# The MLP of a hybrid decoder layer: Strassen's scheme for its up-projection, and a reordered norm phase

## What is computed

```python
def rmsnorm(x, w):
    y = x * lax.rsqrt(jnp.mean(jnp.square(x), axis=-1, keepdims=True) + EPS)
    return y * w

h = concatenate([meta_tokens, x])
mix = hybrid_mixer(rmsnorm(h, norm_mix_pre), w_in, ...)       # starts with rmsnorm(...) @ w_in
h = h + rmsnorm(mix, norm_mix_post)
f = jnp.square(jax.nn.relu(rmsnorm(h, norm_mlp_pre) @ w_mlp_up)) @ w_mlp_down   # 1024 -> 4096 -> 1024
h = h + rmsnorm(f, norm_mlp_post)
return h[:, 16:]
```

## Time and profile before

| | before |
|---|---|
| median of 3 runs | 1740.33 us (1739.41 to 1749.16) |
| the profiled execution's own time | 1749.06 us |
| its span, first to last instruction | 1746.8 us |
| PE busy | 1638.4 us (94%) |
| DVE busy | 821.7 us (47%) |
| POOL busy | 802.8 us (46%) |
| ACT busy | 491.3 us (28%) |
| mean granted TensorE clock | 0.977 of full |

### The profile page before, as it was taken

How to read it: one execution, slowest core, us unless ns; L and a number is a source line. 1 busy time by engine, 2 the same in 40 slices (tenths; PEclk the granted TensorE clock), 3 DMA queues, 4 the chain that set the end, 5 groups by cost and what they waited for, 6 DMA issues and landing times.

```text
span 1746.8 us, 23031 instructions
## 1 busy us (share of the span) xinstructions
PE 1638.4 (94%) x8311; PEld 1402.6 (80%) x8311; DVE 821.7 (47%) x1404; ACT 491.3 (28%) x1002; POOL 802.8 (46%) x775
## 2 busy tenths in 40 slices
PE   2999999987999999789999999999999999999998
PEld 2999998866887878568887778888888888888886
DVE  5465515155666666647778774222222222222226
ACT  4222312233444444345554443020202020101022
POOL 4452544144565643734321315646464646464623
PEclk8999999998999999889999999999999999999999
DMA  5343622226355433578878642111111111111113
GB/s 175 87 123 91 190 72 61 66 74 170 117 152 152 142 116 103 153 248 296 293 277 284 247 145 90 50 49 49 47 51 46 53 43 54 42 54 42 54 67 150
DMA packets 165542, 208.43 MB, mean 119 GB/s; under 512 B 18912, under 2 KB 117056, under 8 KB 165472
## 3 DMA queue, kind: packets, MB, share of 16 engines
q1 hardware_dynamic: 165472, 207.52, 37.2%
HBM read 138.16 MB, written 69.30 MB: 119 GB/s over the span
## 4 chain that ended last, share of the span: by engine, by line
PE 64%; DVE 7%; ACT 2%; DMA 1%; issue 1%; POOL 1%; SPq 0%; DVEq 0%; ACTq 0%
PE ps L2303 20%; PE ps L2289 20%; PE ps L2187 5%; PE ps L1454 4%; PE ps L1380 2%; PE ps L1429 2%; PE ps L1400 1%; DVE pTlo L1625 1%; PE ps L2143 1%; PE ps L1440 1%; PE ps L1426 1%; PE ps L2167 1%; DVE stat L1610 1%; PE ps L1386 1%; PE ps L1427 1%
## 5 line engine op out<-in xcount | busy, mean ns | idle before, releaser
L164 POOL TENSOR_TENSOR ring<-stage,zero 128x512 fp32r<-128x512 f32 (+2 forms) x191 | 207.0, 1084 | 324.2 <-PE ps L2303 108.8
L2303 PE MATMUL ps<-ring,f1hi 128*128 128x512 f32 x1024 | 315.2, 389 | 0.0
L2289 PE MATMUL ps<-hmThi,ring 128*128 128x512 f32 x960 | 299.2, 390 | 3.5 <-DVE ring L2651 3.5
L166 POOL TENSOR_TENSOR ring<-stage,ring 128x512 fp32r<-128x512 f32 (+2 forms) x191 | 250.4, 1311 | 14.9
L2303 PEld LDWEIGHTS ps<-ring,f1hi 128*128 128x128 f32 x1024 | 192.2, 188 | 39.9
L2289 PEld LDWEIGHTS ps<-hmThi,ring 128*128 128x128 f32 x960 | 180.7, 188 | 41.5 <-DVE ring L2651 4.0
L2303 PE MATMUL ps<-ring,f1lo 128*128 128x512 f32 x512 | 199.2, 389 | 0.0
L2668 DVE TENSOR_TENSOR acc<-ps,acc 128x512 f32<-128x512 f32 x128 | 88.0, 691 | 212.1 <-PE ps L2303 210.2
L2289 PE MATMUL ps<-hmTlo,ring 128*128 128x512 f32 x480 | 187.2, 390 | 0.0
L2461 ACT ACTIVATE relu<-ps 128x512 f32<-128x512 f32 x64 | 38.2, 597 | 518.0 <-PE ps L2289 518.0
L2659 DVE TENSOR_TENSOR ps<-ps,relu 128x512 f32<-128x512 f32 x64 | 44.8, 700 | 218.4 <-ACT relu L2461 218.4
(11 more groups left out here) (376 smaller groups left out, 3399.8 us busy)
## 6 DMA issues: line engine op xcount, KB each, us to landing
stage<-w_mlp_up SPq DMA_DIRECT2D x64, 256.0 KB, 2.6
stage<-w_mlp_down SPq DMA_DIRECT2D x64, 256.0 KB, 2.6
stage<-w_in SPq DMA_DIRECT2D x40, 256.0 KB, 2.7
stage<-w_out SPq DMA_DIRECT2D x32, 256.0 KB, 4.5
xt<-x SPq DMA_DIRECT2D x8, 512.0 KB, 7.0
d_xT<-xdT SPq DMA_DIRECT2D x8, 512.0 KB, 3.3
d_x<-x_tok SPq DMA_DIRECT2D x8, 512.0 KB, 4.6
d_zT<-zs SPq DMA_DIRECT2D x16, 256.0 KB, 2.3
```

Of the source, the lines that this page charges most:

```text
L164: pool.tensor_tensor(hi, src, k.zero[:, 0:1].broadcast_to([P, width]), ALU.add).then_inc(k.sem(fam + "_hi"), 1)
L166: pool.tensor_tensor(lo, src, hi.bitcast(F32), ALU.subtract).then_inc(k.sem(fam + "_cut"), 1)
L2289: mm = pe.matmul(ps[:, bank_of(n, first), :], block_w[:, P * j:P * j + P], HM[b][:, kk, at], start=(kk == 0 and a == 0 and b == 0), stop=( ...
L2303: mm = pe.matmul(ps[:, 2 + n % 4, :], f1[a][:, j, P * t:P * t + P], W[b][:, HALF + 2 * j + c, :], start=(j == 0 and a == 0 and b == 0), st ...
```

## The change

**Up-projection.** The first group of 512 features stays as it was. The other 3584 are taken in 14 groups of 256 (`SUB`), a loop of PE in which the up-projection of a group is seven products of quarters (the Winograd form of Strassen's scheme). The weight's quarters are A11, A12, A21, A22 (512 of the width by 128 features), the quarters of the normed input B11 and so on (512 of the width by 512 positions). Each product is 4 slices x 3 passes = 12 matmuls of 512 columns, where eight such products did it before. The sums of weight quarters S1 to S4 are made by POOL for each group, the sums of input quarters T1 to T4 once, by DVE, during the first group (`t2_first` ... `t4_parts`). Banks X, Y, Z, V collect the products; three intermediate results are copied out by ACT (`kept`) and added by DVE (`total`). The down-projection of a group has 16 banks of 2 slices x 3 passes = 6 matmuls. The tiles go in the order 4 to 7, 0 to 3. In the first group the down banks are copied instead of added and their order is changed. The weights of a group are loaded as quarters (256 KB each, in runs of 512 bytes) after the products that use the same place.

**Norm phase.** x tiles are loaded first, five of them ahead of the first weights; the tables that are used later come last. The square's table is loaded with the root's by an early root. ACT scales four of the eight tiles, DVE the other four. The learned positions are turned early. PE works on the projection of f = 0 and of a third of f = 1 between the transposes (`part`) and does the rest of f = 0 before the block ends. POOL cuts 16 blocks there, not 8 (`AHEAD`).

Some semaphores are merged or renamed elsewhere; that moves nothing. The core of the diff:

```diff
-AHEAD = KD
+AHEAD = 2 * KD
@@ phase_norm, scalar
+            for t in ORDER[:FIRST]:
+                square(t)
+            root(0, slice(0, FIRST))
+            square(4)
+            scaled(1)
+            scaled(3)
+            square(5)
+            square(6)
+            high(0)
+            square(7)
+            high(1)
+            root(1, slice(FIRST, NT + 1))
+            high(2)
+            scaled(5)
+            scaled(7)
@@ phase_norm, tensor
+            for n in range(6, 2 * KD):
+                turn(n)
+                if n < 6 + KD:
+                    part(0, 0, n - 6, 0)
+                    part(1, 0, n - 6, 3)
...
+            for q in (1, 2):
+                for kk in range(KD):
+                    mm = part(0, q, kk, q)
@@ phase_rest
+    PRODUCTS = ("A11", "S1", "S2", "S4", "S3", "A12", "A22")
+    BANK_OF = {"A11": X, "S1": Y, "S2": X, "S4": Y, "S3": X, "A12": Z, "A22": X}
+    RESULTS = ((0, 1, Y, "S2"), (1, 1, V, "S1"), (0, 0, Z, "A11"), (1, 0, X, None))
@@ gpsimd
+            def up_quarters(G):
+                scaled(G, "S3", 1)
+                scaled(G, "A22", 2)
...
+                combined(G, "S1", "S3", "A22", ALU.add, 2)
+                scaled(G, "A11", 4)
+                combined(G, "S2", "S1", "A11", ALU.subtract, 4)
+                combined(G, "S3", "A11", "S3", ALU.subtract, 5)
+                scaled(G, "A12", 7)
+                combined(G, "S4", "A12", "S2", ALU.subtract, 7)
+                for n, q in enumerate(PRODUCTS):
+                    pool.wait_ge(sem("x_hi"), of_sub(G, 9, n + 1))
+                    pool.tensor_tensor(mats[q][1][:, :, :], raw(q), mats[q][0][:, :, :].bitcast(F32), ALU.subtract).then_inc(sem("x_lo"), 1)
@@ tensor
+            def product(G, n):
+                q = PRODUCTS[n]
+                pe.wait_ge(sem("x_lo"), of_sub(G, 11, n + 1))
+                if q == "A11":
+                    pe.wait_ge(sem("v_sq_out"), 2 + UP + of_sub(G, 4))
+                if q in ("S1", "S2", "S3", "A22"):
+                    pe.wait_ge(sem("x_tlo"), table(MOVING[q], 1) + 1)
+                if q in ("S2", "S4", "S3"):
+                    pe.wait_ge(sem("x_kept"), of_sub(G, 3, n - 1))
+                if q == "A22":
+                    pe.wait_ge(sem("x_sum"), of_sub(G, 3, 2))
...
+                for kk in range(4):
+                    for a, b in PASSES:
+                        mm = pe.matmul(bank, mats[q][a][:, kk, :], MOVING[q][b][:, kk, :], ...)
-            with pe.Fori(1, GRPS) as g:
-                for n in range(UP):
-                    up_bank(g, n, False)
-                down_group(g)
+            with pe.Fori(FIRST_SUB, SUBS) as G:
+                for n in range(7):
+                    product(G, n)
+                down_sub(G)
@@ scalar
+            def sub(G):
+                weights_high(G)
+                if isinstance(G, int):
+                    for c in range(2):
+                        table_high(T4, c)
+                kept(G)
+                down_high(G)
+                result_high(G)
@@ vector
+            for n in range(11, DN):
+                down_first(n)
+            dve.wait_ge(sem("x_tlo"), table(T2, 1) + 1)
+            for c in range(2):
+                t4_parts(c)
+            for c in range(2):
+                table_low(T4, c)
+            up_sub(FIRST_SUB)
```

More of the change, by code:

```diff
@@ L281, in root, with high @@
                 act.activation(s_[:, part], v[:, part], ACT.Sqrt).then_inc(sem("sqrt"), 1)
-            for t in range(NT // 2):
-                square(t)
-            root(0, slice(0, NT // 2))
-            act.wait_ge(sem("c_in"), 80)
-            after = {1: 4, 3: 5, 4: 6, 5: 7, 7: 8}
-            for n in range(2 * KD):
+            def high(n):
                 half, kk = n // KD, n % KD
@@ new lines, in down_sub @@
+            def down_sub(G):
+                pe.wait_ge(sem("x_lo"), of_sub(G, 11, 11))
+                for n in range(DN):
+                    t, c = TILES[n // 2], n % 2
+                    if n in (0, DN // 2):
+                        pe.wait_ge(sem("v_sq_out"), 2 + UP + of_sub(G, 4, 2 if n == 0 else 4))
+                    pe.wait_ge(sem("v_added"), ADDED + of_sub(G, DN, max(n - 3, 0)))
+                    for j in range(2):
+                        for a, b in PASSES:
+                            mm = pe.matmul(ps[:, 2 + n % 4, :], fs[a][:, j, P * t:P * t + P], half(wd[b][:, j, :], c),
+                                           start=(j == 0 and a == 0 and b == 0), stop=(j == 1 and a == 1))
@@ new lines, in kept, with down_high @@
+            def kept(G):
+                for n, q in enumerate(("A11", "S1", "S2")):
+                    act.wait_ge(sem("v_up"), UP + of_sub(G, 7, n + 1))
+                    act.activation(result_room(1, *KEPT[q]), ps[:, BANK_OF[q], :], ACT.Copy).then_inc(sem("x_kept"), 1)
+            def down_high(G):
+                for j in range(2):
+                    act.wait_ge(sem("x_wd"), of_sub(G, 32, 32))
+                    act.activation(wd[0][:, j, :], wd_plain[:, j, :], ACT.Copy).then_inc(sem("x_hi"), 1)
@@ L2731, in _, with t2_first @@
                 dve.wait_ge(sem(f"m_sent{u}"), 16 * NT // 2)
-            for n in range(FT, UP):
-                square(0, n)
-                for t in {FT: (0, 1), FT + 1: (2, 3), UP - 1: (4, 5, 6, 7)}.get(n, ()):
-                    dve.memset(acc[:, t, :], 0.0).then_inc(sem("acc_set"), 1)
-            dve.wait_ge(sem("acc_set"), NT)
+            def t2_first(c):
+                hi, lo = room(T2, c)
+                step(hi, *whole(1, 1, c), ALU.add)
+                step(lo, *whole(0, 1, c), ALU.add)
@@ new lines, in t13_third, with t4_parts @@
+            def t13_third(c):
+                hi, lo = room(T3, c)
+                step(lo, hi, lo, ALU.subtract, (T3, c))
+            def t4_parts(c):
+                hi, lo = room(T4, c)
+                step(hi, *whole(1, 0, c), ALU.add)
+                step(lo, *(x[:, 2 * c:2 * c + 2, :].bitcast(F32) for x in T2), ALU.add)
+                step(lo, hi, lo, ALU.subtract, (T4, c))
+            square(0, FT)
+            t2_first(0)
+            square(0, FT + 1)
+            t2_second(0)
```

504 lines of the change are left out of this document (370 added, 134 removed).

## The result

| | before | after |
|---|---|---|
| median of the runs compared | 1743.40 us (9 runs, 1739.41 to 1749.16) | 1734.06 us (9 runs, 1728.65 to 1736.14) |
| ratio after to before | | 0.9939, 95% interval 0.9924 to 0.9954 |
| the profiled execution's own time | 1749.06 us | 1732.11 us |
| its span | 1746.8 us | 1730.3 us |
| PE busy | 1638.4 us | 1609.7 us |

By the ratio the change is worth 0.61%, about 10.6 us (8.0 to 13.2); the two medians differ by 9.3. The forecast was a gain of 27.6 us, a time of 1712.7 us and a range from 1702.0 to 1726.0. The prediction was wrong: the gain is there, but well under half of it. Of the 21.4 us by which the time was missed, 3.1 are the base: the forecast started from 1740.33 us, the median of three runs, and nine give 1743.40.

What follows compares the result with a forecast made beforehand. PE was taken to bound the kernel, busy 1638.4 of 1746.8 us. The terms -38.1 + 18.9 + 4.4 + 2.7 - 15.5 = -27.6 us, set against the median 1740.33, gave 1712.7 us, range 1702 to 1726.

Steps and rivals of the forecast that it cites:

- rival of 0.10: Groups of 256: weights come late in every group, POOL-ACT-DMA chain 1 us over its cover, 13 us more, 1725.7; chance 0.10.
- the slower one: Groups of 256: same weight chain, but long, PE waits above 2.1 us in each of 13 groups, slower than before; chance 0.03.
- the T4 wait: First group of 256: PE stands 4.4 us, once, as ACT copies the first product only behind T4's second high part.
- the giving back at the end: Last group's down banks: DVE's chain of 5.10 us a tile sets the pace, so 18.9 us come off the 38.1.
- the clock did rise in the norm phase: Norm phase: PE's first 6.6 us slow, then full clock; rival of a low clock, gain 7 instead of 15.5, chance 0.12.
- products and the half of the down banks that moved, without T4: MLP groups: 168 fewer up matmuls save 38.1 us; the last group of 256 has 21.8 us of down matmuls, not 43.5.
- last product to the end: End of the kernel: 48.8 us from the last product to the end of the span, where it was 51.7.
- T4, wait and clock: First group of 256: PE waits 4.4 us, then loses 2.7 us at a low clock behind the wait.
- norm phase: Start of the kernel: projection goes on at 50 us and comes 15.5 us earlier, with POOL setting the block's end.
- T4 costs nothing: First group of 256: rival, shorter T4 steps or other cover for PE, 7.1 us less, 1705.6; chance 0.12.
- the end at PE's pace: Last tiles: rival, the end goes at PE's pace instead of DVE's, 18.9 us less, 1693.8; chance 0.03.

Runs made afterwards that it cites:

- t4_order: Changed kernel, but in the first group of 256 ACT copies the first product before T4's first high part, the others before its second; 1722.30 us, ratio 0.9876.
- products_alone: Changed kernel with the norm phase, AHEAD and projection's first part of the kernel before; 1738.49 us, ratio 0.9963 to the kernel before.
- pool_later: Changed kernel, but POOL cuts its first block only when DVE has scaled the first half; 1732.48 us, ratio 0.9911 to the kernel before.
- best_b: Changed kernel with t4_order, norm_psum, pool_later, the end's edits of order and PSUM, and AHEAD at 14; 1712.15 us, ratio 0.9798 to the kernel before.
- norm_psum: Changed kernel, but the norm phase's two chains of small DVE instructions take one input from PSUM; 1731.07 us, ratio 0.9906 to the kernel before.
- order and PSUM together: Changed kernel, at the end DVE adds a tile before scaling the previous one, and small instructions take one input from PSUM; 1724.21 us, ratio 0.9867.

## Why the prediction was wrong, point by point

**Kept from it.** What bounds the kernel was read rightly. 168 matmuls went and PE is busy through every group; no weights came late in the groups of 256 (rival of 0.10, and the slower one with it). The place and the mechanism of the T4 wait were right, so was the giving back at the end by DVE's chain, and the clock did rise in the norm phase. The windows of `t4_order`, from the start of `part`, show it:

```profile
33.50:38.50 5.00, 5.00 (x19) 4.87 (x20) 2.59 (x4) 0.69 (x1) 4.84 (x5) 0.50 0.37 105
38.50:48.00 9.50, 9.50 (x69) 9.38 (x68) 4.51 (x6) 4.67 (x7) 9.19 (x9) 0.97 0.40 112
```

19 instructions of PE in 5.0 us at the 1.2 GHz level, then 69 in 9.5 at the 2.4 GHz level. I had let 6.6 us run slow.

**The steps that failed**, against what was measured:

| term | forecast | measured | from |
|---|---|---|---|
| products and the half of the down banks that moved, without T4 | -38.1 + 21.8 = -16.3 | -14.7 | first down matmul to `e_wrow`: 594.8 in `t4_order`, 609.5 before |
| last product to the end | -2.9 (51.7 to 48.8) | -0.6 | 50.9 against 51.5 |
| T4, wait and clock | +7.1 | +9.3 | 604.1 against 594.8 |
| norm phase | -15.5 | -8.8 | first bank of z, means |
| sum | -27.6 | -14.8 | |

The first three terms make -6.0 us, and `products_alone` measured 6.4. The sum leaves 4.2 us to the medians' 10.6, whose interval ends at 13.2; 1.4 of them may be the longer stretch above. The rest isn't settled.

*The norm phase*, the term furthest off, 6.7 us. What lay behind the start of `part` came as forecast: it took PE 21.3 us (21.7 forecast), and POOL ended at 49.37 (49.6). Its start was late, and two things were wrong. I took DVE's small instructions, and the scalings at 0.69, from an execution in which POOL was idle until 17.82, and put them beside a POOL that starts at 9.77. The scaling of the second half stood in those rows at 6.26 for five, 1.25 each, beside POOL: I had the slower price in hand and used the faster. `pool_later` gives 12.31 for the factors where POOL is away, `best_b` 22.15 for the second ones (forecast 22.6), and in `norm_psum`, with the small chains freed, the projection comes at 50.9 (forecast 50). So 3.8 of the 4.7 us by which it was late are shown to be this chain. And 73.88, from which I counted, was a late execution: the same row stood at 71.07, 71.79 and 73.65 in the three others with the norm phase of before, so on the mean of the four 1.3 us earlier. The last 0.7 us are open.

*T4.* I priced six steps at 1.2, and named POOL's low parts as an upper bound of 2 us only. Four of the six met POOL, and that took 3.2. The Trainium skill, "SBUF — State Buffer", section "SBUF: two separate sides", has an instruction of DVE with two SBUF inputs and one of GpSimd that reads SBUF shut each other out for their whole length; the trace agrees (2.20 and 2.27, one after the other), and so does the chain of tiny instructions, where the size of DVE's own work didn't matter. I had cited that rule for T4 alone and had not asked where else DVE and POOL would now meet.

*The end.* The 5.10 us of a tile held, but one tile lost 1.84 us to POOL, and `e_last` took 2.28 instead of 1.95. The trace of before already had such a meeting, and I passed over it:

```profile
1714.12 1.25 DVE L364 TENSOR_TENSOR stat<-stat 128x1 f32<-128x1 f32 x1
```

The same instruction took 0.16 us in the other tiles. Here it ended with POOL's add (1715.37 against 1715.36), and that tile lasted 6.53 us. I had taken all eight tiles at the 5.10 of two in which POOL's add was over before the small instructions came.

*The rate.* 1.6 us are missing over 14 groups. A group took 40.88 us where 180 x 0.2266 are 40.79, which makes 1.3 of them.

**The chances.** "T4 costs nothing" and "the end at PE's pace" were wrong as they stood. A cheap change of order makes the first true and is worth 9.3 us. For the second, order and PSUM together give 7.4 of the 18.9 us: tiles are 3.99 us apart, and PE's pace is 2.72. What was missing among the rivals was one cause that acts in three places at once. I had treated the terms as independent, and a common error in them is what took the time out of the range.

## What to carry to other kernels

When a change moves POOL's work in time, list every instruction of DVE that will now run beside it, the tiny ones too: one with two inputs in SBUF can cost the whole of POOL's running instruction (0.16 us became 1.8). Where such a chain is on the path, one input in PSUM frees it. A stage that hands a bank back must not stand in line behind one whose result is needed only later (here T4, four products on). And where the same code varies by 10 us between executions, take several executions for the base, and look for the stretches that repeat to a few tenths (here those behind the first down matmul): those decide.

## What the runs showed of the hardware that I had not expected

- `tensor_scalar` with its one input and its output in SBUF is held by POOL too: the 128x1024 scaling took 0.69 us free and 1.5 to 1.8 beside POOL, a 128x4 or 128x5 one (L431) 0.17 and 0.5 to 1.3. The Trainium skill, "SBUF — State Buffer", section "Who interferes with whom", lists `tensor_scalar` among the operations that may take the port pair that DVE and GpSimd share; the rows agree.
- The hold goes both ways and in turns. Against T4's steps of 2.2 us POOL's low parts took 2.27 us instead of 1.29; neither engine got ahead of the other.
- PE's idle time of 7.5 us was followed by 4.2 us at the 1.2 GHz level, in which 10 matmuls ran that take 2.27 at the other level, so about 2 us more; with the wait gone the clock stayed at 1.00.
- From the first down matmul of the MLP to its last product all five executions with the MLP of before took 609.5 us, while the stretch ahead of it, from the mark at 447, varied from 632 to 641 among all traces. The spread of the run times is made in the phases between, not in the MLP's loop.
